# A gated-delta layer: the matrix of the inverse turned in 32x32 blocks by VectorE at five of its six levels, and the levels three slots apart instead of four

## The chip, the cores and the metric

The kernel runs on one core of a Trainium2 chip. The metric is the device time of one execution in microseconds (us). TensorE (PE; its weight loads are PEld) multiplies matrices, VectorE (DVE) and ScalarE (ACT) work elementwise on SBUF and PSUM, GpSimd (POOL) elementwise on SBUF, and SyncE (SP) issues the weight transfers. Every engine executes its own list in order; they wait for each other through semaphores alone.

## The reference

One decoder layer on 256 tokens of width 2048, batch 1, all in float32. What matters here:

```
h = rms_norm(x, gain);  h @ w_in -> q,k,v,z of MoBA (8 heads x 128), q,k,v,z of DeltaNet (8 x 128), beta, alpha, two gates
lower = where(strict, einsum('bhnid,bhnjd->bhnij', kb, k) * decay, 0)
tmat  = triangular_solve(eye + lower, eye, unit_diagonal=True)      # the inverse
u, w  = tmat @ vb, tmat @ (kb * exp(g))
...                                                                 # scan over the chunks gives o
merged = sigmoid(gate_a) * (ya @ w_branch_a) + sigmoid(gate_b) * (yb @ w_branch_b)
out = rms_norm(x + merged @ w_out, final_gain)
```

The kernel uses chunks of 128 tokens, two of them, so that a head has two triangular 128x128 matrices to invert. It holds both in one tile, the first in one triangle and the second, flipped, in the other.

## The kernel before

**The dense work.** Each weight tile (a unit: 2 x 128 rows by 512 columns) is brought in by SP as float32 (`w_raw`), rounded by ACT into a high part (`w_hi`, L785) and split by DVE into the remainder (`w_lo`, L1011). PE forms three products for each: L497, L498, L499, each 128x512. The ring holds four units. ACT may write a unit only after PE has used the unit four before it; the splits run three units ahead.

**The slots.** One iteration of the loop belongs to one head and has 24 units. After each half of a unit (6 products) comes a slot, numbered 0 to 47, in which PE may execute a few small operations of the two attention branches. All engines run through the same slot numbers in their own lists. In each slot the order is `dn_step` of the head before (slot number plus 48), `dn_step` of this head, `mo_step`, and then in even slots the split of a weight unit; the two last splits of ACT stand in odd slots. So a DeltaNet step at slot 55 runs in slot 7 of the next iteration. The last head's late steps run between the units of branch A.

**The inverse.** It starts from `v` = identity minus the coupling of neighbours (L1156, L1158, L1162 on DVE in slot 26), and doubles the block size six times (`LEVELS = 6`). One level n before the change:

- slot `S_XT[n]`, PE transposes `v` into PSUM (L564), and DVE multiplies it by a mask of the blocks on the diagonal, `own`, into `xe` (L1171);
- slot `S_Y[n]`, PE multiplies `mt` and `xe` (L569), and ACT copies that to `ysb` (L875);
- slot `S_XY[n]`, PE multiplies `ysb` and `xo` (L574), and DVE subtracts it from `v` (L1174).

POOL prepares `mt` (L428) and `xo` (L430, from `v`). After the last level POOL writes `xf` (L435), and then come S_Y0, S_R1, S_Y1, S_O (PE L577, L580 and L581, L585, L588 and L589) and S_YT: PE transposes the head's output (L593), ACT writes `yb_hi` (L893), DVE writes `yb_lo` (L1196).

**Around it.** In slot 16 PE makes the decays (L547) and DVE subtracts in them (L1100, L1104). In slot 18 (S_TURN) PE transposes q, k and v of this head (L539) into the PSUM tile that the head before has used, and so waits first:

```
if s == S_TURN:
    pe.wait_ge(dn_nat_ready, T * h + T)
    if not first:
        pe.wait_ge(yb_lo_ready, h)
```

The MoBA steps stand in slots 34 (PE L603), 37, 40, 42, 44 and 47; in slot 32 ACT copies that branch's projection, `mo_nat` (L903, twice).

Of the kernel before, what the change touches and what calls it, by code (L numbers as in the profile page):

```python
# [5 lines left out]
ALU = mybir.AluOpType  # L6
# [5 lines left out]
P = 128  # L12
# [22 lines left out]
LEVELS = 6  # L35
# [8 lines left out]

S_DEC, S_TURN, S_CONV, S_SILU, S_KK = 16, 18, 20, 22, 24
S_DEC_FIRST = 20
S_Y = [31, 35, 39, 43, 47, 51]
S_XY = [y + 1 for y in S_Y]
S_XT = [y - 1 for y in S_Y]
S_Y0, S_R1, S_Y1, S_O, S_YT = 55, 57, 59, 61, 65  # L50

# [6 lines left out]
def build(nc, x, norm_gain, w_in, conv_w, a_log, dt_bias, dn_norm_gain, w_a, w_b, w_out,  # L60
          final_gain, out):
    ctx = ExitStack()
    with ctx:
        def sb(name, shape, dt=F32):
            return ctx.enter_context(nc.sbuf_tensor(name, shape, dt))

        def sem(name):
            return ctx.enter_context(nc.semaphore(name))
# [36 lines left out]
        own = sb("own", [P, LEVELS, P])  # L105
# [28 lines left out]
        mt = sb("mt", [P, LEVELS, P])  # L134
        v = sb("v", [P, P])
        v0 = sb("v0", [P, P])
        xe = sb("xe", [P, P])
        xo = sb("xo", [P, P])
        ysb = sb("ysb", [P, P])
        xf = sb("xf", [P, T, P])  # L140
        y = sb("y", [P, T, P])
# [20 lines left out]
        A, B = dn_ps[:, 0:CH], dn_ps[:, CH:2 * CH]  # L162
# [30 lines left out]
            "q_squared", "k_squared", "norm_eps", "norm_inv", "weight_ready", "norm_ready", "qn_ready"))  # L193
        vb_ready, kk_done, kk_ready, mt_ready = sem("vb_ready"), sem("kk_done"), sem("kk_ready"), sem("mt_ready")
        w_ready, v0_ready, v_ready, vT_done = sem("w_ready"), sem("v0_ready"), sem("v_ready"), sem("vT_done")
        xe_ready, xo_ready, xf_ready = sem("xe_ready"), sem("xo_ready"), sem("xf_ready")
        y_done, y_ready, xy_done = sem("y_done"), sem("y_ready"), sem("xy_done")
        y0_done, y0_ready, cross_done, r1_ready, y1_done, y1_ready, o_done = (sem(n) for n in (
# [262 lines left out]
        def _(pe):  # L461
# [69 lines left out]
            def dn_step(s, h, first=False):  # L531
# [5 lines that stand above are left out]
                    for p in range(3):  # L537
                        for t in range(T):
                            mm = pe.transpose(dn_ps[:, (p * T + t) * P:(p * T + t + 1) * P],  # L539
                                              dn_nat[:, t, p * P:(p + 1) * P], ident[:, :])  # L540
                    mm.then_inc(dn_turned, 1)
                if s == (S_DEC_FIRST if first else S_DEC):
                    pe.wait_ge(hs_ready, h + 1)
                    if not first:
                        pe.wait_ge(ya_ready, T * h)
                    for t in range(T):
                        mm = pe.matmul(E[:, t * P:(t + 1) * P], hs[:, C_G + t:C_G + t + 1].to_broadcast([P, P]),  # L547
                                       causal[:, :], start=True, stop=True)
                    mm.then_inc(dec_done, 1)
                if s == S_KK:  # L550
                    pe.wait_ge(convs_ready, 3 * (h + 1))
                    pe.matmul(A, convs[:, 3 * P:4 * P], convs[:, 0:4 * P], start=True, stop=True)  # L552
                    pe.matmul(B[:, 0:2 * P], convs[:, 2 * P:3 * P], convs[:, P:3 * P], start=True, stop=True).then_inc(kk_done, 1)
                    if not first:
                        pe.wait_ge(ya_lo_ready, h)
                    for t in range(T):
                        pe.transpose(C[:, t * P:(t + 1) * P], convs[:, (4 + t) * P:(5 + t) * P], ident[:, :])
                    pe.wait_ge(dsub_ready, 5 * (h + 1))
                    for t in range(T):
                        mm = pe.transpose(E[:, t * P:(t + 1) * P], convs[:, t * P:(t + 1) * P], ident[:, :])  # L560
                    mm.then_inc(nat_done, 1)
                if s in S_XT:
                    pe.wait_ge(v_ready, (LEVELS + 1) * h + S_XT.index(s) + 1)
                    pe.transpose(B[:, 0:P], v[:, :], ident[:, :]).then_inc(vT_done, 1)  # L564
                if s in S_Y:
                    n = S_Y.index(s)
                    pe.wait_ge(xe_ready, LEVELS * h + n + 1)
                    pe.wait_ge(mt_ready, LEVELS * h + n + 1)
                    pe.matmul(A[:, 0:P], mt[:, n, :], xe[:, :], start=True, stop=True).then_inc(y_done, 1)  # L569
                if s in S_XY:  # L570
                    n = S_XY.index(s)
                    pe.wait_ge(y_ready, LEVELS * h + n + 1)
                    pe.wait_ge(xo_ready, LEVELS * h + n + 1)
                    pe.matmul(B[:, P:2 * P], ysb[:, :], xo[:, :], start=True, stop=True).then_inc(xy_done, 1)  # L574
                if s == S_Y0:
                    pe.wait_ge(xf_ready, T * h + 1)
                    pe.matmul(A[:, 0:P], xf[:, 0, :], vb[:, 0, :], start=True, stop=True).then_inc(y0_done, 1)  # L577
                if s == S_R1:
                    pe.wait_ge(y0_ready, h + 1)
                    pe.matmul(B[:, P:2 * P], kk[:, Q00, :], y[:, 0, :], start=True, stop=True)  # L580
                    pe.matmul(B[:, 0:P], kk[:, K01, :], y[:, 0, :], start=True, stop=True).then_inc(cross_done, 1)  # L581
                if s == S_Y1:
                    pe.wait_ge(r1_ready, h + 1)
                    pe.wait_ge(xf_ready, T * h + T)
                    pe.matmul(A[:, P:2 * P], xf[:, 1, :], r1[:, :], start=True, stop=True).then_inc(y1_done, 1)  # L585
                if s == S_O:
                    pe.wait_ge(y1_ready, h + 1)
                    pe.matmul(B[:, 2 * P:3 * P], kk[:, Q01, :], y[:, 0, :], start=True, stop=False)  # L588
                    pe.matmul(B[:, 2 * P:3 * P], kk[:, Q11, :], y[:, 1, :], start=False, stop=True).then_inc(o_done, 1)  # L589
                if s == S_YT:  # L590
                    pe.wait_ge(yb_ready, T * h + T)
                    for t in range(T):
                        mm = pe.transpose(A[:, t * P:(t + 1) * P], yb[:, t, :], ident[:, :])  # L593
                    mm.then_inc(ybT_done, 1)
# [184 lines left out]
        def _(act):  # L779
# [52 lines left out]
            def dn_step(s, h, first=False):  # L832
# [33 lines left out]
                if s == S_KK + 2:  # L866
# [3 lines left out]
                    for t in range(T):  # L870
                        act.activation(vb[:, t, :], C[:, t * P:(t + 1) * P], ACT.Copy,
                                       scale=kn[:, 3, t:t + 1]).then_inc(vb_ready, 1)
                if s in S_Y:
                    act.wait_ge(y_done, LEVELS * h + S_Y.index(s) + 1)
                    act.activation(ysb[:, :], A[:, 0:P], ACT.Copy).then_inc(y_ready, 1)  # L875
# [131 lines left out]
        def _(dve):  # L1007
# [67 lines left out]
            def tables_cumulated():  # L1075
# [12 lines left out]
                dve.tensor_copy(tabs[:, :, C_BETA + 1], C[:, 256:256 + H]).then_inc(tabs_ready, 1)  # L1088
                dve.tensor_copy(tabs[:, :, C_REST], cum[:, 1, 0, :]).then_inc(tabs_ready, 1)

            def dn_step(s, h, first=False):
                if s == (S_DEC_FIRST if first else S_DEC):
                    dve.wait_ge(dec_done, h + 1)
# [60 lines left out]
                if s == S_KK + 2:  # L1154
                    dve.wait_ge(kk_ready, 3 * (h + 1))
                    dve.tensor_tensor(w[:, :], kk[:, K00, :], kk[:, K11, :], ALU.add).then_inc(w_ready, 1)  # L1156
                    dve.wait_ge(w_ready, h + 1)
                    dve.tensor_tensor(v0[:, :], w[:, :], neg1[:, :], ALU.mult).then_inc(v0_ready, 1)  # L1158
                    dve.wait_ge(v0_ready, h + 1)
                    if not first:  # L1160
                        dve.wait_ge(xf_ready, T * h)
                    dve.tensor_tensor(v[:, :], v0[:, :], ident[:, :], ALU.add).then_inc(v_ready, 1)  # L1162

                    dve.wait_ge(q_squared, T * (h + 1))
                    if not first:
                        dve.wait_ge(o_mean, h)
                    dve.tensor_scalar(qn[:, :], ssq[:, :], EPS, EPS * P, ALU.add, ALU.mult).then_inc(qn_ready, 1)
                if s in S_XT:
                    n = S_XT.index(s)
                    dve.wait_ge(vT_done, LEVELS * h + n + 1)  # L1170
                    dve.tensor_tensor(xe[:, :], B[:, 0:P], own[:, n, :], ALU.mult).then_inc(xe_ready, 1)  # L1171
                if s in S_XY:
                    dve.wait_ge(xy_done, LEVELS * h + S_XY.index(s) + 1)
                    dve.tensor_tensor(v[:, :], v[:, :], B[:, P:2 * P], ALU.subtract).then_inc(v_ready, 1)  # L1174
                if s == S_R1:
                    dve.wait_ge(cross_done, h + 1)
                    if not first:
                        dve.wait_ge(y1_done, h)
                    dve.tensor_tensor(r1[:, :], vb[:, 1, :], B[:, 0:P], ALU.subtract).then_inc(r1_ready, 1)
# [178 lines left out]
```

## Time and profile before

| | |
|---|---|
| three runs | 823.16, 823.94, 825.99 us (median 823.94) |
| the profiled execution | 824.77 us, its span 823.1 us |
| TensorE busy | 807.9 us, 98% of the span |
| VectorE, ScalarE, GpSimd busy | 484.0, 410.0, 140.5 us |
| granted TensorE clock, mean | 0.995 of full speed |
| the DMA engines' mean busy share | 59.7% |

The span goes from the first to the last instruction; some 1.7 us of the execution lie outside it. Spans of matmuls overlap in the profile, so what one costs is read from the distance between the starts of its neighbours, not from its duration.

### The profile page before, as it was taken

The page shows a single profiled execution, that of the slowest core. Times are in us where ns is not written, and L with a number is a line of the kernel's source. Part 1 is how long each engine was busy: PE and PEld are TensorE (multiplying, and loading weights), DVE is VectorE, ACT ScalarE, POOL GpSimd, SP SyncE. Part 2 cuts the span into 40 slices and gives each one's busy share as a digit, 9 for nine tenths or more (in the row PEclk, how much of TensorE's full clock was granted, in tenths as well). Part 3 has the DMA queues.
Part 4 walks back from the last instruction along what each step waited for, and adds up shares of the span by engine and source line. Part 5 has one row for each costly group of instructions (what it writes and reads, how often), then busy time and mean ns, then how long its engine had stood idle before and what let it go on. Part 6 is the DMA issues. An engine that isn't in the chain of part 4 may idle for free.

```text
span 823.1 us, 12564 instructions
## 1 busy us (share of the span) xinstructions
PE 807.9 (98%) x3859; PEld 666.3 (81%) x3859; DVE 484.0 (59%) x794; ACT 410.0 (50%) x641; POOL 140.5 (17%) x222
## 2 busy tenths in 40 slices
PE   8899999999999999999999999999999999999996
PEld 7788887888888888878888888888888888888874
DVE  4666448555754664585458456654764566765563
ACT  4564545545544555454545545454555563444441
POOL 9112112110211021102112110211031100001120
PEclk9999999999999999999999999999999999999999
DMA  8856565565656455746565564556454566578652
GB/s 210 231 138 190 139 186 156 172 174 158 178 151 179 129 178 153 193 138 180 152 178 162 153 186 136 180 160 185 137 171 137 183 212 187 182 237 282 196 155 102
DMA packets 179207, 142.15 MB, mean 173 GB/s; under 512 B 10880, under 2 KB 144240, under 8 KB 179056
## 3 DMA queue, kind: packets, MB, share of 16 engines
q1 hardware_dynamic: 179184, 141.85, 59.6%
q8 instruction: 13, 0.21, 0.1%
q14 instruction: 10, 0.08, 0.0%
HBM read 139.72 MB, written 2.10 MB: 172 GB/s over the span
## 4 chain that ended last, share of the span: by engine, by line
PE 91%; DVE 3%; issue 2%; SPq 2%; DMA 1%; ACT 0%; DVEq 0%; POOLq 0%; POOL 0%; ACTq 0%
PE pj L497 27%; PE pj L499 27%; PE pj L498 26%; PE dn_ps L569 1%; PE dn_ps L574 1%; PE dn_ps L552 1%; PE dn_ps L539 1%; DVE w_lo L1011 1%; SPq L269 1%; DVE decay L1100 1%; PE dn_ps L564 1%; DMA w_raw<-in_w_in_dram 1%; SPq L274 1%; SPq L252 1%; PE mo_ps L547 0%
## 5 line engine op out<-in xcount | busy, mean ns | idle before, releaser
L1011 DVE TENSOR_TENSOR w_lo<-w_raw,w_hi 128x1024 fp32r<-128x1024 f32 x251 | 312.9, 1250 | 179.9 <-ACT w_hi L785 179.0
L497 PE MATMUL pj<-w_hi,xt_hi 128*128 128x512 f32 x860 | 356.9, 415 | 3.2 <-DVE w_lo L1011 3.1
L785 ACT ACTIVATE w_hi<-w_raw 128x1024 fp32r<-128x1024 f32 x251 | 264.3, 1058 | 149.9 <-PE pj L499 132.2
L499 PE MATMUL pj<-w_hi,xt_lo 128*128 128x512 f32 x860 | 338.7, 394 | 0.0
L498 PE MATMUL pj<-w_lo,xt_hi 128*128 128x512 f32 x860 | 336.4, 391 | 0.0
L499 PEld LDWEIGHTS pj<-w_hi,xt_lo 128*128 128x128 f32 x860 | 161.8, 188 | 36.6
L497 PEld LDWEIGHTS pj<-w_hi,xt_hi 128*128 128x128 f32 x860 | 162.4, 189 | 33.3 <-issue 3.8
L498 PEld LDWEIGHTS pj<-w_lo,xt_hi 128*128 128x128 f32 x860 | 162.7, 189 | 27.4
L430 POOL TENSOR_TENSOR xo<-v,own 128x128 f32<-128x128 f32 x48 | 44.6, 929 | 232.9 <-DVE v L1174 231.0
L875 ACT ACTIVATE ysb<-dn_ps 128x128 f32<-128x128 f32 x48 | 13.2, 276 | 63.0 <-PE dn_ps L569 63.0
L1174 DVE TENSOR_TENSOR v<-v,dn_ps 128x128 f32<-128x128 f32 x48 | 13.7, 286 | 45.5 <-PE dn_ps L574 44.6
L428 POOL TENSOR_TENSOR mt<-w,levels 128x128 f32<-128x128 f32 x48 | 30.7, 640 | 18.7 <-DVE w L1156 18.7
L454 POOL TENSOR_TENSOR gate<-gate 128x512 f32<-128x512 f32 x6 | 10.2, 1714 | 132.3 <-ACT dn_nat L991 132.3
L1120 DVE SCALAR_TENSOR_TENSOR conv<-dn_ps,hs,conv 128x255 f32<-128x255 f32 (+2 forms) x72 | 29.4, 474 | 0.0
L1171 DVE TENSOR_TENSOR xe<-dn_ps,own 128x128 f32<-128x128 f32 x48 | 13.7, 286 | 25.2 <-PE dn_ps L564 24.9
L930 ACT ACTIVATE gate<-pj,rx 128x512 f32 (+1 forms) x16 | 11.0, 685 | 31.3 <-PE pj L499 31.3
L497 PE MATMUL pj<-w_hi,ya_hi 128*128 128x512 f32 x64 | 25.9, 405 | 0.0
L497 PE MATMUL pj<-w_hi,yb_hi 128*128 128x512 f32 x64 | 25.2, 393 | 0.0
L499 PE MATMUL pj<-w_hi,ya_lo 128*128 128x512 f32 x64 | 25.1, 392 | 0.0
L498 PE MATMUL pj<-w_lo,ya_hi 128*128 128x512 f32 x64 | 25.0, 390 | 0.0
L499 PE MATMUL pj<-w_hi,yb_lo 128*128 128x512 f32 x64 | 25.0, 390 | 0.0
L498 PE MATMUL pj<-w_lo,yb_hi 128*128 128x512 f32 x64 | 24.9, 390 | 0.0
(259 smaller groups left out, 766.0 us busy)
## 6 DMA issues: line engine op xcount, KB each, us to landing
w_raw<-in_w_in_dram SPq DMA_DIRECT2D x384, 256.0 KB, 3.1
w_raw<-in_w_out_dram SPq DMA_DIRECT2D x64, 256.0 KB, 3.7
w_raw<-in_w_branch_a_dram SPq DMA_DIRECT2D x32, 256.0 KB, 3.3
w_raw<-in_w_branch_b_dram SPq DMA_DIRECT2D x32, 256.0 KB, 3.5
gate<-in_x_dram SPq DMA_DIRECT2D x8, 256.0 KB, 5.2
gate<-in_x_dram SPq DMA_DIRECT2D x4, 512.0 KB, 7.2
gate<-in_final_norm_gain_dram SPq DMA_DIRECT2D x1, 1024.0 KB, 8.7
out_dram<-gate SPq DMA_DIRECT2D x1, 768.0 KB, 3.7
```

Source lines behind the costliest of these rows:

```text
L428: pool.tensor_tensor(mt[:, n, :], w[:, :], levels[:, n, :], ALU.mult).then_inc(mt_ready, 1)
L430: pool.tensor_tensor(xo[:, :], v[:, :], own[:, n, :], ALU.mult).then_inc(xo_ready, 1)
L497: pe.matmul(bank[:, t, :], hi[:, k, tok], w_hi[:, slot, cs], start=(k == 0), stop=False)
L498: pe.matmul(bank[:, t, :], hi[:, k, tok], w_lo[:, slot, cs], start=False, stop=False)
L499: mm = pe.matmul(bank[:, t, :], lo[:, k, tok], w_hi[:, slot, cs], start=False, stop=(k == kt_all - 1))
L785: act.activation(w_hi[:, slot, :], w_raw[:, slot, :], ACT.Copy).then_inc(hi_ready, 1)
L875: act.activation(ysb[:, :], A[:, 0:P], ACT.Copy).then_inc(y_ready, 1)
L930: act.activation(gate[:, bass.ds(h, 1), t, :].rearrange("p a n -> p (a n)"), pj[0][:, t, :], ACT.Copy, scale=rx[:, 4 + t:5 + t]).then_inc( ...
L1011: dve.tensor_tensor(w_lo[:, slot, :], w_raw[:, slot, :], w_hi[:, slot, :].bitcast(F32), ALU.subtract).then_inc(lo_ready, 1)
L1120: dve.scalar_tensor_tensor(out=conv[:, p, back:SEQ], in0=u_[:, 0:SEQ - back], scalar=tap, in1=conv[:, p, back:SEQ], op0=ALU.mult, op1=ALU. ...
L1171: dve.tensor_tensor(xe[:, :], B[:, 0:P], own[:, n, :], ALU.mult).then_inc(xe_ready, 1)
L1174: dve.tensor_tensor(v[:, :], v[:, :], B[:, P:2 * P], ALU.subtract).then_inc(v_ready, 1)
```

## The change

The five lower levels (blocks of 2 to 32) need only what stands in the 32x32 blocks on the diagonal of `v` transposed. There DVE now transposes `v` itself, 32x32 block by block, into a new SBUF tile `vt`, right after it has written `v`, and multiplies that by `own`. PE's transpose and its slot stay at the sixth level alone. With that slot gone the levels stand three slots apart, the sixth four, and all that follows stands six slots earlier.

```diff
-S_Y = [31, 35, 39, 43, 47, 51]
+S_Y = [29, 32, 35, 38, 41, 45]
 S_XY = [y + 1 for y in S_Y]
-S_XT = [y - 1 for y in S_Y]
-S_Y0, S_R1, S_Y1, S_O, S_YT = 55, 57, 59, 61, 65
+S_XT = S_Y[-1] - 1
+S_Y0, S_R1, S_Y1, S_O, S_YT = 49, 51, 53, 55, 59
...
-                if s in S_XT:
-                    pe.wait_ge(v_ready, (LEVELS + 1) * h + S_XT.index(s) + 1)
+                if s == S_XT:
+                    pe.wait_ge(v_ready, (LEVELS + 1) * h + LEVELS)
                     pe.transpose(B[:, 0:P], v[:, :], ident[:, :]).then_inc(vT_done, 1)
...
+            def turned_part(n, h, first):
+
+                dve.wait_ge(v_ready, (LEVELS + 1) * h + n + 1)
+                if n or not first:
+                    dve.wait_ge(xe_ready, LEVELS * h + n)
+                dve.transpose(vt[:, :], v[:, :]).then_inc(vt_ready, 1)
+                dve.wait_ge(vt_ready, (LEVELS - 1) * h + n + 1)
+                if n:
+                    dve.wait_ge(y_done, LEVELS * h + n)
+                dve.tensor_tensor(xe[:, :], vt[:, :], own[:, n, :], ALU.mult).then_inc(xe_ready, 1)
...
                     dve.tensor_tensor(v[:, :], v0[:, :], ident[:, :], ALU.add).then_inc(v_ready, 1)
+                    turned_part(0, h, first)
...
-                if s in S_XT:
-                    n = S_XT.index(s)
-                    dve.wait_ge(vT_done, LEVELS * h + n + 1)
-                    dve.tensor_tensor(xe[:, :], B[:, 0:P], own[:, n, :], ALU.mult).then_inc(xe_ready, 1)
+                if s == S_XT:
+                    dve.wait_ge(vT_done, h + 1)
+                    dve.tensor_tensor(xe[:, :], B[:, 0:P], own[:, LEVELS - 1, :], ALU.mult).then_inc(xe_ready, 1)
                 if s in S_XY:
-                    dve.wait_ge(xy_done, LEVELS * h + S_XY.index(s) + 1)
+                    n = S_XY.index(s)
+                    dve.wait_ge(xy_done, LEVELS * h + n + 1)
                     dve.tensor_tensor(v[:, :], v[:, :], B[:, P:2 * P], ALU.subtract).then_inc(v_ready, 1)
+                    if n + 1 < LEVELS - 1:
+                        turned_part(n + 1, h, first)
```

PE's list of the loop before, from the end of slot 16 to S_TURN in slot 18 (L497 to L499 the dense products, L593 the transposes of the head before, L539 those of S_TURN):

```order
L497 MATMUL pj<-w_hi,xt_hi 128x512
L498 MATMUL pj<-w_lo,xt_hi 128x512
L499 MATMUL pj<-w_hi,xt_lo 128x512
L593 MATMUL dn_ps<-ident,yb 128x128 x2
L489 REGISTER_ALU
L497 MATMUL pj<-w_hi,xt_hi 128x512
L498 MATMUL pj<-w_lo,xt_hi 128x512
L499 MATMUL pj<-w_hi,xt_lo 128x512
L497 MATMUL pj<-w_hi,xt_hi 128x512
L498 MATMUL pj<-w_lo,xt_hi 128x512
L499 MATMUL pj<-w_hi,xt_lo 128x512
L534 REGISTER_ALU
```

The same place of the changed kernel (its L499 to L501 are the dense products, L541 the transposes of S_TURN):

```order
L501 MATMUL pj<-w_hi,xt_lo 128x512
L491 REGISTER_ALU
L499 MATMUL pj<-w_hi,xt_hi 128x512
L500 MATMUL pj<-w_lo,xt_hi 128x512
L501 MATMUL pj<-w_hi,xt_lo 128x512
L499 MATMUL pj<-w_hi,xt_hi 128x512
L500 MATMUL pj<-w_lo,xt_hi 128x512
L501 MATMUL pj<-w_hi,xt_lo 128x512
L536 REGISTER_ALU
L541 MATMUL dn_ps<-ident,dn_nat 128x128 x6
```

The transposes of the head before no longer stand one slot ahead of those of this head; they stand in slot 11.

DVE's list before, from slot 32 to slot 36 (`v` of a level, split, `xe` of the next level, split, `v`):

```order
L1174 TENSOR_TENSOR v<-v,dn_ps 128x128
L1010 REGISTER_ALU
L1011 TENSOR_TENSOR w_lo<-w_raw,w_hi 128x1024
L1170 REGISTER_ALU
L1171 TENSOR_TENSOR xe<-dn_ps,own 128x128
L1010 REGISTER_ALU
L1011 TENSOR_TENSOR w_lo<-w_raw,w_hi 128x1024
L1174 TENSOR_TENSOR v<-v,dn_ps 128x128
```

DVE's list of the changed kernel, from slot 30 to the start of slot 33's work and on to `xe` (L1188 writes `v`, L1013 is the split):

```order
L1102 TENSOR_TENSOR xe<-vt,own 128x128
L1012 REGISTER_ALU
L1013 TENSOR_TENSOR w_lo<-w_raw,w_hi 128x1024
L1012 REGISTER_ALU
L1013 TENSOR_TENSOR w_lo<-w_raw,w_hi 128x1024
L1187 REGISTER_ALU
L1188 TENSOR_TENSOR v<-v,dn_ps 128x128
L1095 REGISTER_ALU
L1098 STREAM_TRANSPOSE vt<-v 128x128
L1099 REGISTER_ALU
L1102 TENSOR_TENSOR xe<-vt,own 128x128
```

The `v` of slot 33 now stands behind the splits of slots 30 and 32, and `vt` and `xe` right behind it. ACT's list before, from slot 31 to slot 32 (L875 is `ysb`, L903 `mo_nat`, L785 the split's high part):

```order
L785 ACTIVATE w_hi<-w_raw 128x1024
L875 ACTIVATE ysb<-dn_ps 128x128
L223 REGISTER_ALU
L903 ACTIVATE mo_nat<-pj,rx 128x512
L225 REGISTER_ALU
L903 ACTIVATE mo_nat<-pj,rx 128x512
L785 ACTIVATE w_hi<-w_raw 128x1024
```

The changed kernel has the same rows in this order, but its `ysb` here is the one of slot 32 and not of slot 31, and the split behind it is again the one of slot 32.

## Rows read from the trace of the kernel before

**Rows 1.** The page: busy times; the chain that ended last, by engine.

```profile
PE 807.9 (98%) x3859; PEld 666.3 (81%) x3859; DVE 484.0 (59%) x794; ACT 410.0 (50%) x641; POOL 140.5 (17%) x222
PE 91%; DVE 3%; issue 2%; SPq 2%; DMA 1%; ACT 0%; DVEq 0%; POOLq 0%; POOL 0%; ACTq 0%
```

**Rows 2.** Timeline of PE, a slot with a transpose alone (start, duration, instruction).

```profile
324.09 0.39 PE L499 MATMUL pj<-w_hi,xt_lo 128*128 128x512 f32 x1
324.32 0.27 PE L564 MATMUL dn_ps<-ident,v 128*128 128x128 f32 x1
324.35 0.48 PE L497 MATMUL pj<-w_hi,xt_hi 128*128 128x512 f32 x1
324.66 0.39 PE L498 MATMUL pj<-w_lo,xt_hi 128*128 128x512 f32 x1
```

**Rows 3.** Groups by line: the transposes, and the line's waits in total.

```profile
L564 PE MATMUL dn_ps<-ident,v 128*128 128x128 f32 x48 | 13.0, 271 | 0.0
L539 PEld LDWEIGHTS dn_ps<-ident,dn_nat 128*128 128x128 f32 x48 | 5.2, 140 | 3.9 <-issue 3.8
```

**Rows 4.** Timeline around S_TURN, first head's slot, then the fourth head's slot.

```profile
48.33 0.40 PE L499 MATMUL pj<-w_hi,xt_lo 128*128 128x512 f32 x1
...
49.45 0.40 PE L498 MATMUL pj<-w_lo,xt_hi 128*128 128x512 f32 x1
...
277.31 1.22 DVE L1011 TENSOR_TENSOR w_lo<-w_raw,w_hi 128x1024 fp32r<-128x1024 f32 x1
278.44 0.42 DVE L1196 TENSOR_TENSOR yb_lo<-dn_ps,yb_hi 128x256 f32 x1
278.47 0.39 PE L499 MATMUL pj<-w_hi,xt_lo 128*128 128x512 f32 x1
279.00 0.84 PE L539 MATMUL dn_ps<-ident,dn_nat 128*128 128x128 f32 x6
279.92 0.39 PE L498 MATMUL pj<-w_lo,xt_hi 128*128 128x512 f32 x1
```

**Rows 5.** Timeline of the fourth head, slots 31 to 35, all engines.

```profile
299.30 0.38 PE L569 MATMUL dn_ps<-xe,mt 128*128 128x128 f32 x2
299.72 0.28 ACT L875 ACTIVATE ysb<-dn_ps 128x128 f32<-128x128 f32 x1 [2.03 <-PE dn_ps L569]
300.92 0.38 PE L574 MATMUL dn_ps<-xo,ysb 128*128 128x128 f32 x2
301.03 1.07 ACT L785 ACTIVATE w_hi<-w_raw 128x1024 fp32r<-128x1024 f32 x1
301.34 0.29 DVE L1174 TENSOR_TENSOR v<-v,dn_ps 128x128 f32<-128x128 f32 x1 [1.81 <-PE dn_ps L574]
301.71 0.46 POOL L430 TENSOR_TENSOR xo<-v,own 128x128 f32<-128x128 f32 x1 [4.78 <-DVE v L1174]
302.13 1.53 DVE L1011 TENSOR_TENSOR w_lo<-w_raw,w_hi 128x1024 fp32r<-128x1024 f32 x1 [0.51 <-ACT w_hi L785]
303.92 0.27 PE L564 MATMUL dn_ps<-ident,v 128*128 128x128 f32 x1
305.85 0.39 PE L569 MATMUL dn_ps<-xe,mt 128*128 128x128 f32 x2
```

**Rows 6.** Timeline of DVE and POOL, start of the inverse: SBUF operands alone.

```profile
293.25 0.29 DVE L1158 TENSOR_TENSOR v<-w,neg 128x128 f32<-128x128 f32 x1
293.29 0.57 POOL L428 TENSOR_TENSOR mt<-w,levels 128x128 f32<-128x128 f32 x1 [2.35 <-DVE w L1156]
293.57 0.43 DVE L1162 TENSOR_TENSOR v<-v,ident 128x128 f32<-128x128 f32 x1
293.93 0.15 DVE L1167 TENSOR_SCALAR qn<-ssq 128x2 f32<-128x2 f32 x1
```

**Rows 7.** Timeline of DVE: an operation over three times 128 elements.

```profile
309.94 0.61 DVE L1205 SCALAR_TENSOR_TENSOR sm<-far,hs,mo_ps 128x384 f32<-128x384 f32 x1 [0.63 <-PE mo_ps L610]
```

More of the change, by code:

```diff
@@ L136, in build @@
         v0 = sb("v0", [P, P])
+        vt = sb("vt", [P, P])
         xe = sb("xe", [P, P])
@@ L195, in build @@
         w_ready, v0_ready, v_ready, vT_done = sem("w_ready"), sem("v0_ready"), sem("v_ready"), sem("vT_done")
+        vt_ready = sem("vt_ready")
         xe_ready, xo_ready, xf_ready = sem("xe_ready"), sem("xo_ready"), sem("xf_ready")
```

## The prediction

> **What bounds the kernel now.** I read the page first. TensorE is busy for 98% of the span, and of the chain that ended last 91% are its matmuls [rows 1]. So a change counts by what it takes from PE's own list or by what it makes PE wait for. A busy PE can hide a wait, since matmuls overlap in the profile. So I went on to the timeline and measured distances between starts. The dense products follow each other every 0.23 us [rows 2]. Each small operation between them adds a distance, and I compared it over the eight heads. One kind of operation at one place adds the same in every head, which means that PE waits for nobody there. One place is the exception: the transposes of S_TURN.
>
> In the first head, which has no head before it, 1.12 us lie between the last dense product ahead of S_TURN and the second one behind it. In the fourth head they are 1.45 us [rows 4]: 0.33 us more. The wait in PE's queue stands in the groups too, seven times in all, for every head but the first [rows 3]. The rows show whom it waits for. `yb_lo` of the head before (L1196) stands behind a split on DVE, which began at 277.31. It starts at 278.44 and ends at 278.86, and PE starts at 279.00, when it could have at 278.70 [rows 4].
>
> **The change part by part.**
>
> *Five transposes per head leave PE.* With a transpose alone between them, the product ahead and the second one behind start 0.57 us apart; two plain distances are 0.46 [rows 2]. One transpose costs 0.11 us, far less than its own 0.27. 48 of them stand in the trace [rows 3], 40 go: 40 x 0.11 = 4.4 us.
>
> *S_YT goes from slot 17 to slot 11.* `yb_lo` is then ready some 8 us ahead of S_TURN, and the wait has nothing left to wait for: 7 x 0.33 = 2.3 us. What is late next at S_TURN would be `dn_nat`, but the first head shows S_TURN without the 0.33, and it has that wait too. The steps from S_Y0 to S_YT keep their distances, so their waits stay hidden.
>
> *DVE does more*: five transposes per head, 40 in all, and 40 `xe` from SBUF instead of PSUM. At some 0.3 us for each transpose these are 12 us on an engine that is idle for 41% of the span [rows 1]. Behind it stand the splits, which run three units ahead of PE. They don't wait long enough to matter. So the added work costs only where it lies in the chain of a level.
>
> *The levels come closer.* From S_XY to the next S_Y there are now two slots instead of three. In them DVE must do `v`, `vt`, `xe`. Two plain slots make 3.00 us from one small operation to the next (300.92 to 303.92, [rows 5]). The four distances between the five lower levels have the same list on DVE. `v` starts 0.42 us after S_XY [rows 5], and it lasts 0.29. Then come 0.04 for the semaphore, the transpose T, 0.04, `xe` 0.29, and 0.14 from DVE's end to PE's start (278.86 to 279.00, [rows 4]). That is 1.22 us plus T, so there is room while DVE is free. (The first level has three slots, from `v` in slot 26 to slot 29.)
>
> It isn't free in slot 33. In even slots 32 and 38 ACT now has `ysb` ahead of its split; before, all `ysb` stood in odd slots, behind it. In slot 32 `mo_nat` stands between them too, and DVE's split waits for ACT's, and `v` of slot 33 waits behind DVE's split. The old slot 31 has the same list on ACT, and gives the times. Let S_Y of slot 32 start at 0. `ysb` starts at 0.42, `w_hi` at 1.73 and ends at 2.80, `w_lo` starts at 2.83 [rows 5]. Its 1.53 there is with POOL at work on `mt`; alone it takes 1.22, and the next operation starts 0.09 before its end, as at 278.44 [rows 4]. So `v` runs from 3.96 to 4.25, although its data were there at 2.04. `vt` runs from 4.29 to 4.29 + T, `xe` for 0.29 from 4.33 + T, and PE can start at 4.76 + T.
>
> When would PE be there? S_XY is at 1.62 (299.30 to 300.92), slot 34 at 1.62 + 3.00 less the one slot of 1.38 = 3.24. From the old slot 34 to S_Y of 35 are 1.93 us with a transpose and the four of MoBA, so 1.82 without ours [rows 5]: 5.06. The chain fits if T is at most 0.30.
>
> *What T is.* No block transpose stands in the trace. An operation on two columns takes 0.15 us, one on 128 columns 0.29 [rows 6], one on 384 columns 0.61 [rows 7]. I take 0.29, the row with as many columns, and keep 0.15 and 0.61 as bounds. The Trainium skill ("VectorE: DVE Perf Modes", section "The three transpose paths") gives 311 ns for a 128x128 block transpose in bf16, and an estimate by it would add 0.02 us per head; for float32 it gives nothing, and no row here shows one.
>
> *Contention.* `v` also releases POOL's `xo`, 0.08 us after its end, for 0.46 us [rows 5], and so beside `vt` and `xe`. At the start of the inverse POOL's `mt` runs beside two DVE operations on SBUF. One keeps its 0.29, the next takes 0.43 [rows 6]: 0 or 0.14 us more. `xe` is the second such operation here, and I take 0.14. The Trainium skill speaks against this part of the change ("GPSIMD Engine Reference", section 1, "Specifications"): GpSimd's SBUF interfaces are shared with VectorE, and instructions of VectorE with two SBUF inputs contend with it. The old `xe` read PSUM, the new one reads `vt` and `own`, both in SBUF; rows 6 agree. Without that rule the term would be zero.
>
> With both, PE starts S_Y of slot 35 at 4.76 + 0.29 + 0.14 = 5.19 instead of 5.06: 0.13 us, eight times, 1.0 us.
>
> *The other tight level* is 38 to 41. There `w_hi` follows `ysb` without `mo_nat`, from 0.70 at the latest to 1.77, so `w_lo` runs from 1.80 to 3.02 and `v` starts at 2.93. PE could start at 3.73 + T + 0.14 = 4.16; S_Y of 41 is due at 1.62 + 3.00 = 4.62. Room: 0.46. Level 29 to 32 has 3.00 - 1.36 - T = 1.35 with DVE free, level 35 to 38 has 0.66 us of MoBA matmuls more. `mt` and `xo` are a level ahead on POOL, which is busy for 17% [rows 1].
>
> **The sum.** Against the profiled execution's own span: 823.1 - 4.4 - 2.3 + 1.0 = 817.4 us, or 824.8 - 5.7 = 819.1 with what lies around it. The median of the three runs lies 0.8 us below that execution: 823.9 - 5.7 = 818.2 us.
>
> **The rivals.**
>
> - *The small wait* (forecast): slot 35 waits 0.05 to 0.3 us in each head. 823.9 - 6.7 + 0.4 to 2.4 = 817.6 to 819.6. Chance 0.52.
> - *The chain fits*: T is under 0.2, or POOL and DVE don't meet. For it: the first of the two operations in rows 6 is not slowed. Then 823.9 - 6.7 = 817.2. Chance 0.23.
> - *A slow block transpose, 0.61 us*: float32 may need more than one pass. Slot 35 then waits 0.45 us, slot 41 still not. 817.2 + 3.6 = 820.8. Chance 0.11.
> - *The change does only half of what it can*: another wait takes the place of `yb_lo` at S_TURN, DVE's decays in slot 16 for one. Then the 2.3 us stay: 820.5. Against it speaks the first head. Chance 0.05.
> - *Slower*: one mechanism, the block transpose at over 0.88 us. Slot 35 then waits T - 0.16 and slot 41 T - 0.75, and at T = 0.88 both together eat the 0.84 us that each head gains. At 1.2 us they are 1.04 + 0.45, and 817.2 + 11.9 = 829.1. Only a transpose over three times as long as a 128-column operation would do that. Chance 0.04.
> - *No change within what can be told*, with T near 0.8 or with several of the above: 0.05.
>
> **How the numbers follow.** The three runs spread by 0.34%, and 0.3% (2.5 us) is what a measurement of this kernel can tell from no change. Below 821.5 us it is faster: 0.52 + 0.23 + 0.11 + 0.05 = 0.91. Within: 0.05. Slower: 0.04. The range goes from the case with no wait, and the half microsecond by which a median of few runs moves, 816.6, to the slow transpose, 820.9. It leaves out the last two cases and the ends of the others.
>
> **What the changed profile would show.** L541's weight load has no idle time before it, and the distance at S_TURN is 1.12 us in all heads: right on slot 17. The distances at PE's `Y` (L571) are 0.235 us more than plain ones at all levels but the second. If the third or fifth has more, I misread DVE's queue. At the second (slot 35) the excess is the forecast 0.1 to 0.2. STREAM_TRANSPOSE shows T, and a mean of `xe` (L1102) above 0.29 shows contention. I am wrong if T is far from 0.29, or if S_TURN still waits.

## The result, and the profile after

The changed kernel takes 817.43 us (median of five runs, 815.86 to 818.69), the kernel before 825.17 us in the five runs that it is compared with (823.16 to 826.11). The ratio is 0.9906 with a 95% interval of 0.9885 to 0.9928: faster by 0.7 to 1.2%. The forecast was 818.2 us, with a range of 816.6 to 820.9. Its gain was 5.7 us on 823.9; the measured one is 7.7 us on 825.2.

The page of the changed kernel: busy times, and the chain that ended last.

```profile
PE 800.2 (98%) x3819; PEld 661.5 (81%) x3819; DVE 500.0 (61%) x834; ACT 410.5 (50%) x641; POOL 105.7 (13%) x222
PE 93%; SPq 2%; issue 2%; DVE 1%; DMA 1%; ACT 0%; POOLq 0%; POOL 0%; DVEq 0%; ACTq 0%
```

PE has 40 instructions fewer than in [rows 1] and is still the bound. DVE has 40 more and 16 us more work. POOL has the same 222 instructions and 35 us less work.

The profiled executions differ by 9.0 us (spans of 823.1 and 814.1), more than the medians. A measure that is free of such luck is the distance from one head's S_KK to the next. I call it the period. The chain in order of time shows it, first for the kernel before, then for the changed one (start, length, what; S_KK is L552, then L554):

```profile
288.05 0.86 PE dn_ps L552 x2
...
364.70 0.86 PE dn_ps L552 x2
```

```profile
283.59 0.86 PE dn_ps L554 x2
...
359.29 0.86 PE dn_ps L554 x2
```

76.65 us before, 75.70 us after: 0.95 less, with all seven periods of each of these traces within 0.05 of each other. Seven periods make 6.6 of the 9.0 us, and the part behind the last S_KK gives 0.7. The other 1.6 lie ahead of the first S_KK, where the kernels do the same. These are stretches of both, at the start, with each engine's busy time and then the granted clock; first before, then after:

```profile
27.20:30.60 3.40, 3.40 (x10) 2.52 (x9) 3.14 (x4) 1.99 (x4) 0.00 (x0) 0.51 1.06 256
```

```profile
27.20:30.60 3.40, 3.40 (x19) 2.79 (x18) 2.82 (x5) 2.31 (x5) 0.00 (x0) 1.00 1.17 294
```

The clock stood at 0.51 of full speed (1.2 instead of 2.4 GHz) in the first, and PE made 10 matmuls where it made 19 in the second. That is luck of the execution: just before, PE had been idle for much the same time in both, waiting for a split (2.53 us before, 2.63 us after). The change itself is worth the 7.3 us of periods and tail.

At S_TURN of the fourth head the changed kernel has this on PE (L499 to L501 the dense products):

```profile
274.36 0.39 PE L501 MATMUL pj<-w_hi,xt_lo 128*128 128x512 f32 x1
274.59 0.82 PE L541 MATMUL dn_ps<-ident,dn_nat 128*128 128x128 f32 x6
...
275.48 0.40 PE L500 MATMUL pj<-w_lo,xt_hi 128*128 128x512 f32 x1
```

From 274.36 to 275.48 are 1.12 us, the first head's figure in [rows 4]. The fourth head had 1.45 there. It is 1.12 in all eight heads now.

Slots 32 to 35 of the fourth head, DVE's and POOL's work and what it waits for, answer to [rows 5]:

```profile
296.58 0.38 PE L571 MATMUL dn_ps<-xe,mt 128*128 128x128 f32 x2
297.00 0.28 ACT L877 ACTIVATE ysb<-dn_ps 128x128 f32<-128x128 f32 x1 [3.38 <-PE dn_ps L571]
297.17 1.26 ACT L905 ACTIVATE mo_nat<-pj,rx 128x512 f32<-128x512 f32 x2
298.31 1.07 ACT L787 ACTIVATE w_hi<-w_raw 128x1024 fp32r<-128x1024 f32 x1
299.41 1.23 DVE L1013 TENSOR_TENSOR w_lo<-w_raw,w_hi 128x1024 fp32r<-128x1024 f32 x1 [3.02 <-ACT w_hi L787]
300.55 0.28 DVE L1188 TENSOR_TENSOR v<-v,dn_ps 128x128 f32<-128x128 f32 x1
300.87 0.31 DVE L1098 STREAM_TRANSPOSE vt<-v 128x128 f32<-128x128 f32 x1
300.91 0.46 POOL L432 TENSOR_TENSOR xo<-v,own 128x128 f32<-128x128 f32 x1 [5.60 <-DVE v L1188]
301.21 0.31 DVE L1102 TENSOR_TENSOR xe<-vt,own 128x128 f32<-128x128 f32 x1
301.33 0.51 POOL L430 TENSOR_TENSOR mt<-w,levels 128x128 f32<-128x128 f32 x1
301.57 0.30 PEld L571 LDWEIGHTS dn_ps<-xe,mt 128*128 128x128 f32 x2 [0.22 <-DVE xe L1102]
301.63 0.43 PE L571 MATMUL dn_ps<-xe,mt 128*128 128x128 f32 x2
```

`v` starts 3.97 us after S_Y (forecast 3.96), behind the split that waits for `mo_nat`. PE starts the next S_Y at 5.05 (forecast without a wait 5.06). `xe` ends at 4.94. PE's weight load for that product waits 0.22 us for `xe` and starts 0.05 after its end, the matmul 0.06 later; it takes 0.43 instead of 0.38. From the dense product ahead to the second one behind, this S_Y adds 0.28 us in every head, the other levels' 0.23 to 0.24. So there is a wait, and it costs 0.05 us. The two new groups, one line each (duration least, median, most):

```profile
L1098 DVE STREAM_TRANSPOSE vt<-v x40: 311/311/313, 63.1 to 612.9; 128x128 f32<-128x128 f32 x40
...
L1102 DVE TENSOR_TENSOR xe<-vt,own x40: 306/308/314, 63.4 to 613.2; 128x128 f32<-128x128 f32 x40
```

The block transpose takes 0.31 us in float32. The Trainium skill ("VectorE: DVE Perf Modes", section "The three transpose paths") gives the same 311 ns for bf16. `xe` takes 0.31 where I had 0.29 + 0.14.

### The profile page after: what moved, and what is told of

Same layout as the page of the kernel before. It is cut to its first block, busy times and chain, and to the rows that moved or that the text cites. A ratio compares the mean times of both kernels' runs of the same rounds, so it can differ in the third digit from the quotient of the medians.

```text
span 814.1 us, 12609 instructions
## 1 busy us (share of the span) xinstructions
PE 800.2 (98%) x3819; PEld 661.5 (81%) x3819; DVE 500.0 (61%) x834; ACT 410.5 (50%) x641; POOL 105.7 (13%) x222
## 4 chain that ended last, share of the span: by engine, by line
PE 93%; SPq 2%; issue 2%; DVE 1%; DMA 1%; ACT 0%; POOLq 0%; POOL 0%; DVEq 0%; ACTq 0%
PE pj L499 28%; PE pj L501 28%; PE pj L500 27%; PE dn_ps L571 1%; PE dn_ps L576 1%; PE dn_ps L554 1%; SPq L271 1%; PE dn_ps L541 1%; DMA w_raw<-in_w_in_dram 1%; SPq L254 1%; SPq L276 1%; PE mo_ps L549 0%; PE mo_ps L605 0%; PE mo_ps L612 0%; PE dn_ps L555 0%
## 5 line engine op out<-in xcount | busy, mean ns | idle before, releaser
L1013 DVE TENSOR_TENSOR w_lo<-w_raw,w_hi 128x1024 fp32r<-128x1024 f32 x251 | 310.4, 1243 | 189.9 <-ACT w_hi L787 189.2
L499 PE MATMUL pj<-w_hi,xt_hi 128*128 128x512 f32 x860 | 354.0, 412 | 2.9 <-DVE w_lo L1013 2.9
L501 PE MATMUL pj<-w_hi,xt_lo 128*128 128x512 f32 x860 | 337.5, 392 | 0.0
L501 PEld LDWEIGHTS pj<-w_hi,xt_lo 128*128 128x128 f32 x860 | 161.4, 188 | 35.9
L499 PEld LDWEIGHTS pj<-w_hi,xt_hi 128*128 128x128 f32 x860 | 162.1, 188 | 32.0 <-issue 3.5
L432 POOL TENSOR_TENSOR xo<-v,own 128x128 f32<-128x128 f32 x48 | 22.2, 462 | 158.5 <-DVE v L1188 156.7
L1188 DVE TENSOR_TENSOR v<-v,dn_ps 128x128 f32<-128x128 f32 x48 | 13.7, 286 | 25.2 <-PE dn_ps L576 25.2
L430 POOL TENSOR_TENSOR mt<-w,levels 128x128 f32<-128x128 f32 x48 | 25.0, 521 | 18.7 <-DVE w L1169 18.7
L420 POOL TENSOR_TENSOR dn_z<-dn_z,dn_gain 128x256 f32<-128x256 f32 x8 | 5.9, 743 | 162.1 <-ACT dn_z L860 162.1
L499 PE MATMUL pj<-w_hi,ya_hi 128*128 128x512 f32 x64 | 25.5, 399 | 0.0
L499 PE MATMUL pj<-w_hi,yb_hi 128*128 128x512 f32 x64 | 25.2, 393 | 0.0
L501 PE MATMUL pj<-w_hi,ya_lo 128*128 128x512 f32 x64 | 25.0, 391 | 0.0
L501 PE MATMUL pj<-w_hi,yb_lo 128*128 128x512 f32 x64 | 24.9, 390 | 0.0
L571 PEld LDWEIGHTS dn_ps<-xe,mt 128*128 128x128 f32 x96 | 17.5, 188 | 5.2 <-DVE xe L1102 1.8
```

The lines of the kernel that those rows point to most:

```text
L430: pool.tensor_tensor(mt[:, n, :], w[:, :], levels[:, n, :], ALU.mult).then_inc(mt_ready, 1)
L432: pool.tensor_tensor(xo[:, :], v[:, :], own[:, n, :], ALU.mult).then_inc(xo_ready, 1)
L499: pe.matmul(bank[:, t, :], hi[:, k, tok], w_hi[:, slot, cs], start=(k == 0), stop=False)
L501: mm = pe.matmul(bank[:, t, :], lo[:, k, tok], w_hi[:, slot, cs], start=False, stop=(k == kt_all - 1))
L1013: dve.tensor_tensor(w_lo[:, slot, :], w_raw[:, slot, :], w_hi[:, slot, :].bitcast(F32), ALU.subtract).then_inc(lo_ready, 1)
```

## The experiments

Theory: PE is the bound, and the change gives it back two things, five transposes and the wait at S_TURN, and takes a little at slot 35. Rivals: the gain is in the closer levels themselves, or transposes and waits are worth something else than their distances in one trace. All figures of one table:

| kernel | period, us | against the kernel that it is built on | time, median us | ratio to the kernel before (95%) |
|---|---|---|---|---|
| before | 76.65 | | 824.7 (18 runs) | |
| changed | 75.70 | | 817.43 | 0.9906 (0.9885 to 0.9928) |
| e1: before, S_YT earlier | 76.34 | -0.31 | 823.63 | 0.9988 (0.9976 to 0.9999) |
| e2: changed, old slots | 76.03 | -0.62 (to before) | 819.93 | 0.9947 (0.9930 to 0.9964) |
| e3: changed, S_YT late | 76.03 | +0.33 | 820.05 | 0.9947 (0.9928 to 0.9965) |
| e4: changed, `vt` made twice | 76.13 | +0.43 | 820.71 | 0.9948 (0.9930 to 0.9966) |
| e5: changed, PE's transposes kept | 76.30 | +0.60 | 822.52 | 0.9976 (0.9964 to 0.9987) |
| e6: changed, `mo_nat` later | 75.65 | -0.05 | 815.84 (one run) | |
| e7: changed, all six levels | 75.61 | -0.09 | 816.35 | 0.9903 (0.9884 to 0.9923) |
| e8: e6 and e7 | 75.57 | -0.13 | 816.33 | 0.9901 (0.9882 to 0.9920) |
| e9: before, levels three slots apart | 79.12 (three of 80.7) | +2.47 | 849.90 | 1.0309 (1.0292 to 1.0326) |

The period is the usual one of the seven. It resolves 0.02 us a head, the times hardly 1.6 us. Each ratio is against runs of the kernel before that were made together with that kernel's own: 5 for the changed one, 18 for e1 to e4, 13 (median 824.65) for e5, e7 and e8, 7 (824.71) for e9.

**e1_yt_earlier**: the wait at S_TURN alone.

```diff
-S_Y0, S_R1, S_Y1, S_O, S_YT = 55, 57, 59, 61, 65
+S_Y0, S_R1, S_Y1, S_O, S_YT = 55, 57, 59, 61, 63
```

> The kernel before with S_YT alone moved from 65 to 63 (slot 15 of the next iteration). The distance from one head's S_KK to the next is 76.65 us before. My theory: the wait of S_TURN for yb_lo goes and nothing else changes, so the distance at S_TURN falls from 1.45 to 1.12 us, the period to 76.32 us, and the time by 2.3 us (0.3%). Rival 1 (another wait takes its place, DVE's decays for one): period stays 76.65. Rival 2 (the 0.33 us are the price of six transposes at that place and no wait): period stays 76.65 too, but with PE's weight load idle as before.

The distance at S_TURN is 1.12 us in all heads, and the period falls by 0.31. PE's weight loads of that line no longer wait for anybody:

```profile
L539 PEld LDWEIGHTS dn_ps<-ident,dn_nat 128*128 128x128 f32 x48 | 5.7, 140 | 1.0
```

In [rows 3] they had 3.9 us of idle time ahead of them. Within the loop both rivals fall: the step was late and nothing takes its place.

The time fell by only 1.1 us (824.7 to 823.6; the interval allows 0.1 to 2.0) where 2.3 was expected. The trace shows why, at S_YT of the last head, which runs behind the loop:

```profile
657.15 0.39 PE L499 MATMUL pj<-w_hi,ya_lo 128*128 128x512 f32 x1
657.72 0.61 DVE L1191 SCALAR_TENSOR_TENSOR yb<-dn_ps,ro,dn_z 128x128 f32<-128x128 f32 x2 [0.89 <-POOL ro L396]
658.38 0.44 PE L593 MATMUL dn_ps<-ident,yb 128*128 128x128 f32 x2 [0.84 <-DVE yb L1191]
658.58 0.47 PE L497 MATMUL pj<-w_hi,ya_hi 128*128 128x512 f32 x1
658.89 0.39 PE L498 MATMUL pj<-w_lo,ya_hi 128*128 128x512 f32 x1
```

PE waits for `yb`. From the product ahead to the second one behind are 1.74 us, where the seven heads ahead of it have 0.68, as have all eight of the kernel before. So e1 gains seven times 0.31 and loses 1.06 once: 1.1 us in all, what the times say. e1 leaves only two slots between S_O and S_YT. The change keeps four, and has 0.68 us there in all eight heads.

**e2_old_slots**: the block transposes alone.

```diff
-S_Y = [29, 32, 35, 38, 41, 45]
+S_Y = [31, 35, 39, 43, 47, 51]
...
-S_Y0, S_R1, S_Y1, S_O, S_YT = 49, 51, 53, 55, 59
+S_Y0, S_R1, S_Y1, S_O, S_YT = 55, 57, 59, 61, 65
```

> The changed kernel with the slots of before (levels four slots apart, S_Y0 to S_YT at 55 to 65): block transposes by VectorE alone. My theory: five PE transposes of 0.112 us leave each head and the wait at S_TURN stays, so the period is 76.65 - 0.56 = 76.09 us and the time falls by 4.5 us (0.54%); PE waits for no xe. Rival (the gain is the closer levels, and the transposes cost PE little): period above 76.4 us. Together with e1 it should make the change's whole 0.95 us a head less the small wait; what is missing from 0.95 then comes from the closer levels.

The period is 76.03, 0.62 less, 0.12 for each transpose. The wait at S_TURN is there (1.45 us in seven heads). e1 and e2 add up to 0.93 of the change's 0.95. So the levels three slots apart give and cost nearly nothing in themselves (0.05 us for the wait of slot 35, and about as much back, below). e3, with the close levels and the late S_YT, has the same period. The close levels serve to bring S_YT forward without bringing it nearer to S_O. Moving S_YT alone by two slots does that in the loop too, but pays for it at the last head (e1).

**e3_yt_late**: the change with S_YT put back.

```diff
-S_Y0, S_R1, S_Y1, S_O, S_YT = 49, 51, 53, 55, 59
+S_Y0, S_R1, S_Y1, S_O, S_YT = 49, 51, 53, 55, 65
```

> The changed kernel with S_YT alone put back to 65 (slot 17). My theory: the wait at S_TURN comes back whole, period 75.70 + 0.33 = 76.03 us, time 2.3 us above the changed kernel, 0.6% under the kernel before. Rival (S_TURN no longer waits since DVE is otherwise placed): period 75.70.

As forecast: 76.03, and the wait is there to the full. The step from slot 59 to 65 takes 0.33 us a head, whatever the levels do.

```profile
L541 PEld LDWEIGHTS dn_ps<-ident,dn_nat 128*128 128x128 f32 x48 | 5.2, 140 | 3.9 <-issue 3.8
```

**e4_turned_twice**: how much room the chains have.

```diff
                 dve.transpose(vt[:, :], v[:, :]).then_inc(vt_ready, 1)
-                dve.wait_ge(vt_ready, (LEVELS - 1) * h + n + 1)
+                dve.wait_ge(vt_ready, 2 * (LEVELS - 1) * h + 2 * n + 1)
+                dve.transpose(vt[:, :], v[:, :]).then_inc(vt_ready, 1)
+                dve.wait_ge(vt_ready, 2 * (LEVELS - 1) * h + 2 * n + 2)
```

> The changed kernel with VectorE's block transpose of v into vt made twice, one after the other with a semaphore between, at all five levels: each chain is 0.31 + 0.04 = 0.35 us longer. My theory: only the level of slot 35 has no room (in the changed kernel xe ends 0.11 us ahead of PE's start there, 0.81 at slot 41, 1.6 or more elsewhere), so S_Y of slot 35 starts 0.35 us later, the period is 76.05 us, the time 2.8 us above the changed kernel. Rival (slot 41 is tight too): 76.1 to 76.4 us. Rival (DVE's work is hidden): 75.70.

It grows by 0.43 instead of 0.35, all of it at slot 35: slot 41 keeps 0.38 us between `xe`'s end and PE's start. The timeline of the fourth head's slots 33 to 35 shows the rest:

```profile
303.91 0.31 DVE L1098 STREAM_TRANSPOSE vt<-v 128x128 f32<-128x128 f32 x1
303.95 0.47 POOL L432 TENSOR_TENSOR xo<-v,own 128x128 f32<-128x128 f32 x1 [5.66 <-DVE v L1190]
...
304.25 0.31 DVE L1100 STREAM_TRANSPOSE vt<-v 128x128 f32<-128x128 f32 x1
304.27 1.05 ACT L787 ACTIVATE w_hi<-w_raw 128x1024 fp32r<-128x1024 f32 x1
304.37 0.47 POOL L430 TENSOR_TENSOR mt<-w,levels 128x128 f32<-128x128 f32 x1
304.60 0.39 DVE L1104 TENSOR_TENSOR xe<-vt,own 128x128 f32<-128x128 f32 x1
305.04 0.49 PE L571 MATMUL dn_ps<-xe,mt 128*128 128x128 f32 x2 [0.21 <-DVE xe L1104]
```

`xe` here starts while POOL's `mt` has 0.24 us to go, and takes 0.39 us, 0.08 more than in the changed kernel. Neither transpose is slowed beside POOL. So the contention that I had put at 0.14 exists, and it falls on the two-input operation. It is no price per operation, nor does it go by the time that POOL is at work beside it, for POOL works beside the whole of `xe` in the changed kernel. In every row `xe` ends 0.15 us behind the POOL operation that was running when it started:

| where | left of POOL's operation when VectorE's starts | POOL's ends at | VectorE's ends at | length of VectorE's |
|---|---|---|---|---|
| changed, slot 35 | 0.16 us of `xo` | 301.37 | 301.52 | 0.31 |
| e4, slot 35 | 0.24 us of `mt` | 304.84 | 304.99 | 0.39 |
| before, [rows 6] | 0.29 us of `mt` | 293.86 | 294.00 | 0.43 |

Without POOL beside it `xe` takes 0.293 us (e7, sixth level). The `mt` that starts in the changed kernel while `xe` runs does not lengthen `xe`.

**e5_pe_turns_kept**: the transposes' price on PE at another place.

```diff
                     pe.wait_ge(mt_ready, LEVELS * h + n + 1)
+                    if n < LEVELS - 1:
+                        pe.transpose(B[:, 0:P], v[:, :], ident[:, :])
```

> The changed kernel with PE's transpose of v into PSUM kept at the five lower levels, right ahead of the level's product, though nobody reads it. My theory: each costs PE 0.112 us wherever it stands, so the period is 75.70 + 0.56 = 76.26 us and the time 4.5 us above the changed kernel. Rival (a transpose is free beside a small product that stands next to it, and the old cost was that of breaking the dense sequence once more): period below 75.9.

0.60 for five, 0.12 each, right beside another small product. The timeline (first level of the fourth head): L573 starts 0.11 us after L572.

```profile
293.19 0.40 PE L501 MATMUL pj<-w_hi,xt_lo 128*128 128x512 f32 x1
293.42 0.27 PE L572 MATMUL dn_ps<-ident,v 128*128 128x128 f32 x1
293.53 0.39 PE L573 MATMUL dn_ps<-xe,mt 128*128 128x128 f32 x2
```

It costs what it did in a slot of its own. The rival falls: an extra break of the dense sequence costs nothing beside the operation itself.

**e6_mo_nat_later**: what makes slot 33 late.

```diff
-                if s == M_TURN - 2:
+                if s == M_TURN - 1:
                     if not first:
                         act.wait_ge(pv_done, h)
```

> The changed kernel with ACT's mo_nat in slot 33, behind the split of slot 32, instead of slot 32. My theory: mo_nat is what makes the split, and so v of slot 33, late; v then starts at about 2.9 us instead of 3.98 after S_Y of slot 32, and the 0.05 us that S_Y of slot 35 costs more than the others goes: period 75.65 us, time 0.4 us less. Rival (the 0.05 us have another cause): period 75.70 with v earlier. If MoBA's transposes in slot 34 then wait for mo_nat, the period is longer than 75.70.

`v` starts 2.82 us after S_Y instead of 3.97, and the period is 75.65. S_Y of slot 35 now adds the same distance as the others. The small wait of the changed kernel was 0.05 us, and this was its cause. MoBA's transposes did not wait.

**e7_all_levels** and **e8_all_and_mo_nat**: the versions that follow.

```diff
-                if s == S_XT:
-                    pe.wait_ge(v_ready, (LEVELS + 1) * h + LEVELS)
-                    pe.transpose(B[:, 0:P], v[:, :], ident[:, :]).then_inc(vT_done, 1)
...
                 dve.transpose(vt[:, :], v[:, :]).then_inc(vt_ready, 1)
+                done = (LEVELS + 2) * h + n + 1
+                if n == LEVELS - 1:
+                    dve.wait_ge(vt_ready, done)
+                    dve.transpose(vt[32:64, 0:32], v[0:32, 32:64]).then_inc(vt_ready, 1)
+                    dve.transpose(vt[64:96, 96:128], v[96:128, 64:96]).then_inc(vt_ready, 1)
+                    done = done + 2
...
-                    if n + 1 < LEVELS - 1:
+                    if n + 1 < LEVELS:
```

> The changed kernel with the sixth level's transpose on VectorE too: there the mask keeps, of the blocks off the diagonal, only one in each half of 64, so two more 32x32 transposes with input and output in different partitions fill them; PE has no transpose of v left. All slots as in the changed kernel. My theory: PE sheds another 0.112 us a head, DVE has room from slot 42 to slot 45 (over 4 us for some 1.2 us of work): period 75.59 us, time 0.9 us under the changed kernel, about 1.1% under the kernel before. Rival (moving blocks across partitions is slow on DVE and makes S_Y wait or splits late): period above 75.70.

> The two edits together: all six levels turned by VectorE, and mo_nat in slot 33. My theory: both gains add, period 75.54 us, time 1.3 us under the changed kernel, 1.1% under the kernel before. Rival: as for each alone.

e8 is this and the edit of e6. The periods are 75.61 and 75.57: 0.09 and 0.13 less than the changed kernel. The two small transposes of e7, which move a block to other partitions as they turn it, are cheap:

```profile
L1099 DVE STREAM_TRANSPOSE vt<-v x8: 201/201/202, 87.4 to 616.7; 32x32 f32<-32x32 f32 x8
L1100 DVE STREAM_TRANSPOSE vt<-v x8: 205/206/206, 87.7 to 617.0; 32x32 f32<-32x32 f32 x8
```

Both beat the kernel before by some 1%. Against the changed kernel the gain is 0.7 and 1.1 us by periods, and the times don't resolve it: the intervals of all three overlap widely.

**e9_pe_three_slots**: the closer levels without the block transposes.

```diff
-S_Y = [31, 35, 39, 43, 47, 51]
+S_Y = [31, 34, 37, 40, 43, 46]
...
-S_Y0, S_R1, S_Y1, S_O, S_YT = 55, 57, 59, 61, 65
+S_Y0, S_R1, S_Y1, S_O, S_YT = 51, 53, 55, 57, 61
```

> The kernel before, with PE's transposes at all six levels, and only the levels three slots apart: S_Y = 31, 34, 37, 40, 43, 46, and S_Y0 to S_YT at 51, 53, 55, 57, 61. Now PE's transpose of v stands one slot behind the product that v comes from. My theory: closer levels are worth only the wait at S_TURN (0.33 us a head), and here they cost far more. In slot 34 ACT has ysb, moT and mo_z ahead of its split, DVE's split waits for it, and v of slot 35 waits behind DVE's split, until some 4.65 us after S_Y of slot 34, where PE wants to transpose it at about 3.7. Period 76.65 - 0.33 + 1.1 = 77.4 us, more if the levels of slots 40 to 41 wait too; the time is 6 us or more above the kernel before. Rival (PE's list has room for three slots too, and the block transposes matter only by the 0.112 us each): period 76.3 us, 2.3 us under the kernel before.

Slower, as expected, but by 25 us where I had put 6 or more. The wait that I had worked out, at the transpose of slot 36, is 0.62 us where I had 1.1. A larger one stands at slot 42, which I had not worked out. This is the second half of it in the first head:

```profile
88.43 0.19 ACT L917 ACTIVATION_READ_ACCUMULATOR prob<-sm,mx 128x1 f32 x1
88.52 1.04 ACT L785 ACTIVATE w_hi<-w_raw 128x1024 fp32r<-128x1024 f32 x1
88.61 0.40 PE L499 MATMUL pj<-w_hi,xt_lo 128*128 128x512 f32 x1
89.59 1.22 DVE L1011 TENSOR_TENSOR w_lo<-w_raw,w_hi 128x1024 fp32r<-128x1024 f32 x1 [4.87 <-ACT w_hi L785]
90.73 0.28 DVE L1174 TENSOR_TENSOR v<-v,dn_ps 128x128 f32<-128x128 f32 x1
...
91.07 0.33 PE L564 MATMUL dn_ps<-ident,v 128*128 128x128 f32 x1 [2.06 <-DVE v L1174]
```

ACT comes to its split only after `ysb` and the whole softmax of slot 40. DVE's split waits for it, `v` waits behind DVE's split, and PE waits 2.3 us for `v` in every head. And PE's idle time costs once more. The first of these stretches holds the wait, the second is 3.4 us that begin some 1.5 us after it, the third the next 4 us (the granted clock is the number before the DMA share):

```profile
88.00:92.50 4.50, 2.44 (x14) 1.75 (x13) 1.79 (x4) 2.30 (x7) 0.88 (x2) 1.00 0.07 12
92.50:95.90 3.40, 3.40 (x11) 2.73 (x10) 1.23 (x1) 1.92 (x3) 0.00 (x0) 0.50 0.51 145
95.90:100.00 4.10, 4.10 (x24) 3.49 (x23) 2.23 (x5) 0.00 (x0) 0.46 (x1) 0.99 0.43 122
```

After three of the eight waits the clock is at 0.50 for 3.4 us, and those periods are 1.6 us longer (80.7 instead of 79.1). So levels three slots apart are not free to take: with PE's transposes they make the kernel 3% slower, and with VectorE's they cost 0.05 us a head.

## Why the prediction was right

The direction, the mechanism and the places were right, and the gain of 5.7 us was 1.6 us short of the 7.3 that the periods and the tail show. That the forecast time came within 0.8 us all the same is luck in part: it was counted from a median of three runs of the kernel before (823.9), and the five runs that it was compared with have 825.2. By its steps:

- **Five transposes leave PE, 4.4 us.** Right, and a little small. e2 gives 0.62 us a head, which is 4.9 us for eight. Of the excess over 5 x 0.112, 0.04 us a head lie in the dense products: the mean of the plain distances between them falls from 229.4 to 229.2 ns when the transposes go (some 235 of them in a period). Why was not tried.
- **S_TURN's wait, 2.3 us.** Right. Seven times 0.31 (e1) to 0.33 (e3), and no other wait came in its place. That S_YT kept its distance from S_O mattered: e1, which shortens it, pays 1.06 us at the last head.
- **The small wait of slot 35, 1.0 us.** Right in place and cause (e6), wrong in size: 0.05 us a head, 0.4 in all. It was the sum of two terms. T was 0.31 where I had 0.29. Contention was the mis-sized one: 0.02 us instead of 0.14. I had carried over 0.14 from rows 6 as a fixed price, but there `mt` had 0.29 us to go when `v` started. Here `xo` has 0.16 to go, since `vt` runs first, and e4 with 0.24 to go has 0.09 (both against 0.293 without POOL). With 0.31 and 0.02 the working gives 5.09 against 5.06, 0.03 us, where 0.05 was measured. The Trainium skill's rule ("GPSIMD Engine Reference", section 1, "Specifications") is that VectorE instructions with two SBUF inputs contend with GpSimd. The traces agree, 0.02 to 0.14 us; that section gives no size.
- **Slot 41 has room.** Right: 0.81 us between `xe` and PE, and still 0.38 with the transpose made twice.
- **Everything else is hidden.** Right for the engines that I named. I had not seen that POOL gains: `xo` takes 0.46 us in every level now, on an engine that nobody waits for.
- **The sum.** With the measured terms it is 4.9 + 2.2 - 0.4 = 6.7 us. Periods and tail make 7.3. Of the 0.6 us between, 0.5 lie within the periods: 0.62 + 0.31 - 0.05 = 0.88 us a head by the terms, 0.95 measured. Most of these 0.07 us are in distances that the edit does not touch: the dense products' mean is 229.1 ns in the changed kernel (0.04 to 0.06 us a head), and the product of S_XY adds 0.228 us on average instead of 0.232 (0.02 us). What makes them shorter stays open. The medians' 7.7 us are within their interval of both.

The measured wait of 0.05 us is the lower edge of the forecast case. The case "the chain fits" (817.2 us) is only 0.4 us away, far below what the times can tell, but neither of its conditions held: T is not under 0.2, and POOL and DVE do meet. The slow block transpose, the half effect and the slower case are excluded by T = 0.31 and by S_TURN.

## What to carry to other kernels

When the bound engine's list is regular, measure each small operation by the distance that it adds between its neighbours, and compare the same place over all iterations. A place where one iteration is shorter shows a wait that no table of waits names well. Before moving steps closer, follow the in-order queue of each helper engine slot by slot. What made steps late here was never their own work but a bulk operation of even slots, and behind it a copy on a third engine. And a freed slot is worth most where it moves a step away from one that has to wait for it: here a third of the gain came from two constants' distance. Where the last iteration's late steps run outside the loop, look there too when a constant moves: e1's period gains 0.31 us seven times, and one wait behind the loop takes half of it back.

## What the runs showed of the hardware

- VectorE's block transpose of 128x128 float32 takes 0.311 us, and one of a single 32x32 block, from 32 partitions to 32 others, 0.20 us. Two such blocks and one whole turn replaced PE's full transpose where the mask keeps few blocks.
- GpSimd and VectorE's operations with two SBUF inputs hold each other up, and the one that starts first keeps its length. Started second, a VectorE operation is longer by what is left of GpSimd's, less some 0.14 us: by 0.02, 0.09 and 0.14 us in the table at e4, and by 0.31 for the split of 1.53 us in [rows 5], which starts with 0.45 us of an `mt` to go. Started second, GpSimd's operation ends some 0.32 us behind VectorE's: the `mt` of [rows 6] does, the `mt` at 301.33 of the changed kernel, and `xo` here, third level of the second head before, behind the split. The profile's spans on POOL are rough; VectorE's lengths don't rest on them. The first line is the `mt` beside the split of [rows 5]:

```profile
302.13 0.46 POOL L428 TENSOR_TENSOR mt<-w,levels 128x128 f32<-128x128 f32 x1
...
154.80 1.22 DVE L1011 TENSOR_TENSOR w_lo<-w_raw,w_hi 128x1024 fp32r<-128x1024 f32 x1
154.96 1.37 POOL L430 TENSOR_TENSOR xo<-v,own 128x128 f32<-128x128 f32 x1 [5.67 <-DVE v L1174]
```

  At three of the six levels before `xo` took 1.37 to 1.45 us in this way, 0.46 at the others, 0.93 on average. In the changed kernel it always starts ahead of `xe` and keeps its length:

```profile
L432 POOL TENSOR_TENSOR xo<-v,own 128x128 f32<-128x128 f32 x48 | 22.2, 462 | 158.5 <-DVE v L1188 156.7 <-DVE v L1175 1.8
```

- A transpose of 128x128 between dense float32 products costs PE 0.11 to 0.12 us, less than half of its 0.27 us in the profile, alone in a slot or beside another small product.
- In e9 the granted clock fell to half for 3.4 us after three of the eight waits in which PE was idle for 2.06 us, and not after the other five. At the start of the program it fell after 2.53 us of idle time in the kernel before, and not after 2.63 us in the changed one.
